# Conditioning sums over partitions: from columns, one matmul per 128 outputs, to rows, two matmuls per group of 512

## The reference, cut to what matters

```python
mod = silu(c) @ w_ada[i] + b_ada[i]        # 1024 x 6144, for the tokens
mod_c = silu(c_ctx) @ w_ada[i] + b_ada[i]  # the same weights, for the context
sh1, sc1, g1, sh2, sc2, g2 = split(mod, 6)
h = rms_norm(x) * (1 + sc1) + sh1
x = x + g1 * mixer(h)                      # layer 0: short convolution, layer 1: attention
h = rms_norm(x) * (1 + sc2) + sh2
x = x + g2 * swiglu(h)                     # layer 2: experts in its place
```

## Time and profile before

| | us |
|---|---|
| median of three runs | 2145.72 (2136.67, 2145.72, 2147.68) |
| the profiled execution | 2139.97 |
| its span, first to last instruction | 2138.2 |
| TensorE busy | 2032.2 (95%) |
| VectorE busy | 701.9 (33%) |
| mean granted TensorE clock | 0.981 |

### The profile page before, as it was taken

One profiled execution on the slowest core, in us unless ns is written; L12 is line 12 of the kernel. 1 busy time (PEld: TensorE's weight loads), 2 busy tenths in 40 slices (PEclk: granted clock), 3 DMA queues, 4 the chain that ended last, 5 costly groups with the idle time before them and its releaser, 6 DMA issues.

```text
span 2138.2 us, 23891 instructions
## 1 busy us (share of the span) xinstructions
PE 2032.2 (95%) x9774; PEld 1213.8 (57%) x9774; DVE 701.9 (33%) x1261; ACT 277.3 (13%) x573; POOL 115.6 (5%) x158
## 2 busy tenths in 40 slices
PE   6999889999999989988999999989988899999998
PEld 2444434444444446445788888768877544454444
DVE  2566323423440224427243412475432300000001
ACT  2000020000000011125100001233121200000000
POOL 0001000000000002000011101130000000000000
PEclk9999999999999999999999999999999999999999
DMA  9423354423322143001676535042024799999997
GB/s 401 165 79 109 147 211 143 158 98 132 132 79 81 66 199 136 0 0 40 258 284 240 192 143 224 1 172 90 3 81 165 307 428 428 428 430 428 428 429 318
DMA packets 48761, 419.91 MB, mean 196 GB/s; under 512 B 5440, under 2 KB 5456, under 8 KB 22960
## 3 DMA queue, kind: packets, MB, share of 16 engines
q1 hardware_dynamic: 29376, 344.73, 39.7%
q0 software_dynamic: 18880, 71.18, 9.4%
q10 hardware_dynamic: 432, 2.95, 0.4%
HBM read 417.79 MB, written 1.05 MB: 196 GB/s over the span
## 4 chain that ended last, share of the span: by engine, by line
PE 82%; DVE 7%; DMA 7%; ACT 2%; issue 1%; DVEq 0%; ACTq 0%; SPq 0%; POOLq 0%
PE PS L851 18%; PE PS L868 11%; PE PS L1037 8%; PE PS L1165 8%; PE PS L880 5%; DMA ring<-w_moe 5%; PE PS L1218 4%; PE PS L1025 4%; PE PS L1185 4%; PE PS L1198 3%; DVE SC L1544 2%; PE PS L995 2%; PE PS L898 2%; PE PS L825 2%; PE PS L1006 2%; PE PS L832 1%
## 5 line engine op out<-in xcount | busy, mean ns | idle before, releaser
L851 PE MATMUL PS<-A,ring 128*128 128x512 f32 (+1 forms) x1408 | 466.3, 492 | 9.2 <-ACT A L513 9.2
L851 PEld LDWEIGHTS PS<-A,ring 128*128 128x128 f32 x1408 | 269.9, 193 | 193.9 <-issue 173.3
L868 PE MATMUL PS<-A,ring 128*128 128x512 f32 (+1 forms) x704 | 228.6, 486 | 3.2 <-DVE A L1603 3.2
L1037 PE MATMUL PS<-ring,A 128*64 128x512 f32 x1024 | 223.6, 593 | 3.7 <-DMA ring<-w_moe 2.9
L868 PEld LDWEIGHTS PS<-A,ring 128*128 128x128 f32 x704 | 133.3, 190 | 96.1 <-issue 87.1
L1165 PE MATMUL PS<-A,ring 128*128 128x512 f32 x384 | 167.9, 598 | 2.0 <-ACT A L513 2.0
L1037 PEld LDWEIGHTS PS<-ring,A 128*64 128x64 f32 x1024 | 73.9, 137 | 150.1 <-issue 141.6
L1544 DVE SCALAR_TENSOR_TENSOR SC<-A,CS,SC 128x512 f32<-128x512 f32 x208 | 143.7, 745 | 5.1 <-DMA A<-ada 2.9
L1165 PEld LDWEIGHTS PS<-A,ring 128*128 128x128 f32 x384 | 73.0, 192 | 91.4 <-issue 89.7
L1603 DVE TENSOR_TENSOR A<-A,PS 128x512 f32 (+1 forms) x44 | 24.4, 554 | 304.3 <-ACT A L522 304.3
L880 PE MATMUL PS<-A,ring 128*128 128x256 f32 (+1 forms) x384 | 113.7, 458 | 8.5 <-DMA ring<-w_cout 6.7
(11 more groups left out here) (309 smaller groups left out, 1885.3 us busy)
## 6 DMA issues: line engine op xcount, KB each, us to landing
ring<-w_moe SPq DMA_DIRECT2D x96, 2048.0 KB, 18.4
ring<-w_fin SPq DMA_DIRECT2D x44, 1024.0 KB, 7.7
ring<-ada POOLq DMA_DIRECT2D x64, 512.0 KB, 3.8
A<-ada POOLq DMA_DIRECT2D x64, 512.0 KB, 3.8
ring<-w_fout SPq DMA_DIRECT2D x16, 1408.0 KB, 6.1
ring<-w_conv SPq DMA_DIRECT2D x8, 1536.0 KB, 12.9
ring<-w_qkv SPq DMA_DIRECT2D x6, 2048.0 KB, 16.0
ring<-w_win SPq DMA_DIRECT2D x6, 2048.0 KB, 11.3
```

The source lines that it names most:

```text
L851: mm = pe.matmul(PS[:, 2 * (s % 3) + half, 0:T], slot(stage, s, k * 256 + half * 128, k * 256 + half * 128 + 128), h_of(k, T), start=(k == ...
L868: mm = pe.matmul(PS[:, s, 0:T], slot(stage, s, k * 128, k * 128 + 128), HID[:, k * T:(k + 1) * T], start=(k == 0), stop=(k == KF - 1))
L1037: mm = pe.matmul(PS[CAP * e:CAP * (e + 1), g, :], XG[:, k * P + e * CAP:k * P + (e + 1) * CAP], slot("moe", k // 2, w, w + 512), start=(k ...
```

## The change

`ada_sum` now streams `ACC` and uses as weights a window of 12 columns of a constant that has ones in one column: a new constant `row`, 23 columns wide, one at index 11. The window for group g has its column of ones at 11 - g, so the sum of group g's 512 columns comes out as one row on a partition, and zeros are added to the other rows. The host hands over the groups of each layer in reverse order, so the row's number is that of its 512 outputs. Two matmuls a group: for two conditions one each, 512 columns, on partitions from 0 and from 32; for layer 2 one for each half of the 512 columns. All accumulate in bank 6 without a start flag, so VectorE clears rows 0 to 63 of the bank beforehand (`ada_open`). When a layer's groups are done VectorE copies the rows to SBUF (`ada_close`, tile `SUMS`), and TensorE spreads them to columns with four matmuls (`ada_spread`): 128 columns of the rows are the weights, and columns of the identity are streamed. The spread of layer 0 stands behind product 3 of cout; those of layers 1 and 2 behind the last product of the down stage. `ada` waits for the spread; for layers 1 and 2 it moves from chunk 6 of `residual` to behind chunk 7. TensorE's `Fori` loops of two turns in `ffn` become written-out code.

```diff
+ ("row", 23)                                  # constants
+ SUMS = SC[0:64, 0:GRP]
- def ada_sum(l, g, it=0, per_turn=0):
+ def ada_sum(l, g):
-     for m in range(4):
-         for c in range(conds):
-             col = (g * 4 + m) * 2 + (1 if l == 2 else c)
-             col = bass.ds(it * (8 * per_turn) + col, 1) if per_turn else slice(col, col + 1)
-             mm = pe.matmul(PS[:, 6, col], ACC[:, c, m * P:(m + 1) * P], ones[:, 0:1], start=True, stop=True)
+     o = COFF["row"] + g - (PE_G if l == 0 else 0)
+     pick = C[:, o:o + NG]
+     for i in range(2):
+         a, b = (0, GRP) if conds == 2 else (i * GRP // 2, (i + 1) * GRP // 2)
+         mm = pe.matmul(PS[32 * i:32 * i + NG, 6, a:b], pick, ACC[:, i if conds == 2 else 0, a:b], start=False,
+                        stop=False, skip_group_check=True)
      mm.then_inc(sem("ada_mm"), 1)
+ def ada_spread(l):
+     pe.wait_ge(sem("rows_copied"), 3 + l)
+     out = PS[:, 6, 0:8 * NG].rearrange("p (g m c) -> p m c g", m=4, c=2)
+     row = ident[0:64, 0:64].rearrange("p (c g) -> p c g", c=2)[:, :, 0:NG]
      for m in range(4):
+         cs = (0, 2) if l < 2 else (m // 2, m // 2 + 1)
+         mm = pe.matmul(out[:, m, 0:2, :] if l < 2 else out[:, m, 1:2, :], SUMS[:, m * P:(m + 1) * P],
+                        row[:, cs[0]:cs[1], :], start=True, stop=True)
      mm.then_inc(sem("ada_mm"), 1)
  def ffn(l):
-     with pe.Fori(0, 2) as it:                # both loops
+     for it in range(2):
...
+     ada_spread(l + 1)                        # at its end
  def out_proj(stage, rhs_of, T):
+         if stage == "cout" and m == 3:
+             ada_spread(0)
+ def ada_open():
+     dve.memset(PS[0:64, 6, :], 0.0)
+ def ada_close(l):
+     dve.wait_ge(sem("ada_mm"), PG_BASE[l + 1] + 1 + l)
+     dve.tensor_copy(SUMS, PS[0:64, 6, :]).then_inc(sem("rows_copied"), 1)
  def residual(i):
          if stage in ("fout0", "fout1") and m == 6:
-             ada(layer + 1, 0, 48, (2 * layer + 2, 2 * layer + 3))
+             ada_close(layer + 1)
...
+     if stage in ("fout0", "fout1"):
+         ada(layer + 1, 0, 48, (2 * layer + 2, 2 * layer + 3))
  def ffn_in(l):
+     ada_open()
+ ada_open()                                   # ahead of the conv loop
+ ada_close(0)                                 # behind it
```

## The result

The changed kernel takes 2130.87 us (median of nine runs, 2124.76 to 2135.65), the kernel before 2145.1 in the same comparison (nine runs, 2136.67 to 2147.68). The ratio is 0.9938, with a 95% interval of 0.9920 to 0.9956: 13.3 us faster. Run again beside the experiments it was 2134.55 against 2143.41, ratio 0.9949 (0.9930 to 0.9969). The forecast was 2128.

The account below looks back on a forecast made before the run. TensorE was taken to bound the kernel (busy 95% of the span, 82% of the chain). Sums removed -19.7, spreads +2.0, cout +2.8 make -14.9 us, from 2142.8 to 2128 us; range 2118 to 2143.

Parts of the forecast that it names:

- Which groups count: Sums on TensorE's path: 19 of the 20 groups for two conditions and 11 of layer 2's 12 save time.
- The price of a group: Sum group for two conditions: 1.05 us with edges of 0.09 and 0.10, 0.76 less than before; bounds 0.96 to 1.19.
- The second rival: Sum groups: TensorE drains in full at each edge, leaving 10.7 us faster, 2132 us; chance 0.10.
- Layer 2's groups: Gate, up and down products of layer 1: each sum saves 0.48 us, 11 of them 5.3 us (3.3 to 6.6).
- the shorter weight load: Ahead of the first matmul of a layer 2 sum: the weight load takes 85 ns and not 192.
- the down products: Layer 1's down products: their two layer 2 sums priced like those in gate and up, 0.48 us less each.
- The loops: TensorE's unrolled two-turn loops: no turn costs anything now, so writing them out gains nothing.
- The spreads: Three times four matmuls, 1.0 us each (0.8 to 1.2); the two after down stages add 2.0 us on the path.
- The cout chain: Before product 4 of the conv stage's output projection: 1.8 us wait plus 1.0 spread, 2.8 us added (2.3 to 5.5).
- Three steps in place of two: A group's two matmuls don't start together: group 1.48 us, kernel 4.5 us faster, 2138 us; chance 0.08.
- The straightened code: Four stages written out: 14 instruction packets each make TensorE wait 2.5 us, kernel 20 us slower, 2163; chance 0.05.
- The third rival: No overlap of accumulating matmuls in bank 6: group 1.91 us, kernel 6 us slower, 2149 us; chance 0.06.

Follow-up runs that it names:

- the pair on the same columns: Changed kernel with both matmuls of each group on partitions 0 to 11, so on the same array columns: 2159.08 us, ratio 1.0065 to the kernel before.
- the doubled pair: Changed kernel with each group's two matmuls issued twice in a row: 2158.52 us, ratio 1.0057 to the kernel before.
- four blocks: Changed kernel with each group's sums in four matmuls on partitions 0, 32, 64 and 96, copy and spread over 128 rows: 2119.91 us, ratio 0.9882.
- The shifted kernels: Kernel before, and the same with TensorE's loops written out, each with the eight matmuls of `ada_columns` issued twice: 2143.18 and 2143.26 us.

## Why the prediction was right

**Which groups count, and that they run side by side.** Right, and shown: the pair on the same columns loses 0.86 us a group, the doubled pair costs one pair's streaming.

**The price of a group.** Forecast 1.05 us with two conditions, measured 1.19. The streaming is exact (0.86); the term that was mis-sized is the edges, 0.19 forecast and 0.33 measured. The 0.09 and 0.10 were read to the next pass's start, and the third loss, in the step after that start, was not looked for. That is 19 x 0.14 = 2.7 us less gain. The first period was to be 28.5 and is 28.63. The second rival put 0.14 more on a group, with a chance of 0.10, and its size is what was measured. The Trainium skill's page "TensorEngine Tiling (Array Packing)", Key Properties, says that changing the tiling mode drains the TensorE. Whether the 0.33 are a drain or late weight loads the rows don't decide; the doubled pair shows that they hang on the change and not on the pairs, and the spreads that a change of rows has an edge as well as one of columns (0.1 us ahead of a spread with weights of 64 rows, none with 128).

**Layer 2's groups.** Forecast 0.48 less each, period 14.64; measured 14.67 to 14.68, so 0.44, of which 0.08 is the loops'. So the narrow sum itself gives 0.36. From the sum's start to the next product it is 0.54 (1086.06 to 1086.60), and 0.53 was forecast; what failed is the 0.11 for the shorter weight load, since with the loops written out the sum follows VectorE's end after 0.04 us with either width. And the two in the down products can't be priced alike: there TensorE doesn't wait for VectorE, and a sum of the kernel before costs 0.81 us (1237.56 to 1238.37) with no edge ahead of it. The new one costs 0.54 and 0.10 ahead of it, so the two save 0.3 us and not 1.0.

**The loops.** "No turn costs anything now and none is to be won" was half right. No turn costs anything; something ahead of each of layer 2's sums does, 0.08 us, where the sum waits for VectorE. It goes with the loops; that it is the register work which computes the column is argued and not shown.

**The spreads.** Forecast 1.0 us each, measured 0.99, and 0.93 for a repeated one. On the path, as said. The 0.1 ahead of each was not in the forecast.

**The cout chain.** Forecast 2.8 us with the spread. From product 2's start at 243.51 to product 4's at 260.04 it is 16.53 us, of which 32 x 0.429 = 13.73 are products, 2.80. The sum is exact and its terms are not: the wait is 1.6 and not 1.8, the spread 1.0, and 0.2 are the edges behind the sum and ahead of the spread. The clock was taken to be untouched (nearest to the wait at 625.40) and that failed in this kernel: 1.7 us more (29.40 - 27.70), inside the bounds given. With four blocks the same stall left it at 1.00, so the row chosen was not wrong in kind; the outcome isn't fixed by the length of the stall.

**The sum.** By the rows of the two profiles: the conv stage's six groups 6 x 0.62 = 3.7 less, cout's one and fout0's two 1.9, fin0's ten 6.2, fin1's nine 4.0, fout1's two 0.3: 16.1 removed, where 19.7 were forecast and 15.5 with the drains. Added: two spreads 2.2, cout 2.7 (the edge behind the sum is counted with its group) and its clock 1.7: 6.6. That leaves 9.5; the spans differ by 10.2, and the medians by 13 to 14; the fit at equal clock says 12.5. Forecast 14.9. The other 0.7 is a small balance of large terms in stretches whose instructions didn't change. The first conv product starts 1.9 us later (45.38 against 43.45). Cout's first two products took 0.9 less (15.57 against 16.49). From fin0's first product to fout0's, 1.0 us more went than the groups explain, and from fin1's first to fout1's 3.8 more; there the pieces behind the second sum ran at 1.00 (1072 to 1086 us), in the kernel before at 0.90 (1080 to 1097). From the last feed-forward's norm on it is 2.8 us more (2128.0 - 1290.4 against 2138.2 - 1303.5), of which 3.3 arise in one place: at 1432 us the changed kernel had a clock of 0.59, where the kernel before had 1.00 in the same matmuls (L1312 to L1322 there), and from the first of them to the next product it is 9.78 us against 6.45. So part of the agreement of 2128 with 2130.87 is luck: the groups' gain was forecast 3.6 us too high, the clock in cout cost 1.7 that were put at none, and other stretches differed in both directions by up to 3.8. The middle of the kernel before was taken at 2142.8, and its nine runs gave 2145.1.

```profile
1432.00:1440.00 8.00, 8.00 (x22) 6.02 (x22) 6.26 (x9) 3.18 (x9) 0.00 (x0) 0.59 0.00 1
```

```profile
1444.00:1451.00 7.00, 7.00 (x37) 5.95 (x36) 3.70 (x3) 3.78 (x9) 0.00 (x0) 1.00 0.16 63
```

The first is the changed kernel, the second the kernel before. What stays open is why one idle time is followed by a lower clock and another of the same length is not. The shifted kernels suggest that it moves with the schedule; what rule it follows they don't show.

**The rivals.** Three steps in place of two would have given 28.9 in fin0, and four blocks no gain; the rows have neither. The straightened code costs nothing measurable: the kernel with the loops written out is not slower, and 6 instruction packets came in fin0's stretch. The third rival took the matmuls of L799 and L1037 to start fresh; in the code these too accumulate, with the start flag on the first of eight blocks alone, so the doubt was smaller than it looked. Its mechanism didn't occur, but brought about with the same columns it gave the slowdown it was priced at, and more.

## What to carry to other kernels

To sum over partitions into few outputs, make the long operand the moving one and give each matmul its own block of 32 PSUM partitions: the weights are then a dozen columns, and up to four such matmuls cost the time of one. Price a group by its streaming plus what it costs to change the shape of the weights and back (0.33 us here, with one pair between or two), so gather narrow work into few places. And where a result has to go round through another engine before a waiting product, put it one product ahead of the need: the stall was 1.5 us, and in the stage's rows it cost 3.4 with the clock, though the whole kernel's times don't tell the two apart.

## What the runs showed of the hardware

- Two matmuls on partitions 0 and 32 that accumulate in one bank without a start flag run side by side: four passes of 512 columns in 0.96 us, 1.82 on the same columns. Four on partitions 0, 32, 64 and 96: eight passes of 256 columns in 0.55.
- A change between weights of 128 columns and of 12, and back, costs 0.33 us in all around a group of 512-column passes. Weights of 64 rows and 128 columns among those of 128 rows have such edges too: eight passes cost 1.1 us with them and 0.81 with 128 rows.
- The granted clock behind a stall of 1.53 us was 0.94 over 30 us in the changed kernel and 1.00 over 28 us with four blocks; behind another of 1.53 us in the changed kernel, ahead of fout0, it was 1.00 over 35 us.
- A run's time goes with its mean granted clock, 1.6 us per 0.001. An edit that only shifts later work by 2 us didn't show as slower, and writing out loops looked like 0.25% with an interval that excludes zero. A verdict on a change of half a percent needs the clock beside it.
